# Three of sixteen weight units per feed-forward input step get their low parts from an accumulating DMA

## The reference

```python
h = rms_norm(x, norm_ffn[l])
gate_up = jnp.einsum('btd,df->btf', h, w_ffn_in[l])     # w_ffn_in: 2048 x 11264
ff_gate, ff_up = jnp.split(gate_up, 2, axis=-1)
x = x + jnp.einsum('btf,fd->btd', jax.nn.silu(ff_gate) * ff_up, w_ffn_out[l])
```

## Time and profile before

| | us |
|---|---|
| median of 3 runs | 2148.68 |
| lowest, highest run | 2147.15, 2149.55 |
| profiled execution, span of its instructions | 2146.8 |
| PE busy, all instructions | 2135.6 (99%) |
| DVE busy | 1742.5 (81%) |
| ACT busy | 1261.2 (59%) |
| POOL busy | 138.1 (6%) |

### The profile page before, as it was taken

The page is one execution under the profiler, slowest core; times in us unless marked ns, Lnnn a source line. Parts: engine busy times, 40 slices in busy tenths (PEclk is TensorE's granted clock), DMA queues, the critical chain, the costliest instruction groups (busy, mean ns, idle before and its releaser), DMA issues.

```text
span 2146.8 us, 30208 instructions
## 1 busy us (share of the span) xinstructions
PE 2135.6 (99%) x10176; PEld 1788.8 (83%) x10176; DVE 1742.5 (81%) x2125; ACT 1261.2 (59%) x1483; POOL 138.1 (6%) x218
## 2 busy tenths in 40 slices
PE   9999999999999999999999999999999999999998
PEld 9988888888888888888888888888888888888886
DVE  6578788666565698999899887787889999999886
ACT  6465455465544665555555555557667666666565
POOL 2022433101000000000000000000000000000000
PEclk9999999999999999999999999999999999999999
DMA  7666555575555566666666666666666666656664
GB/s 254 182 189 211 157 157 150 174 236 174 183 186 181 186 205 199 198 196 198 203 188 196 200 193 199 192 204 187 206 206 187 188 193 194 193 180 208 203 193 152
DMA packets 211513, 412.35 MB, mean 192 GB/s; under 512 B 13176, under 2 KB 13280, under 8 KB 211296
## 3 DMA queue, kind: packets, MB, share of 16 engines
q1 hardware_dynamic: 208608, 402.70, 60.9%
q0 software_dynamic: 1920, 5.31, 0.8%
q10 hardware_dynamic: 896, 3.15, 0.5%
HBM read 409.01 MB, written 3.16 MB: 192 GB/s over the span
## 4 chain that ended last, share of the span: by engine, by line
PE 96%; DVE 2%; DMA 1%; ACT 0%; issue 0%; DVEq 0%; SPq 0%; ACTq 0%
PE gp L1983 49%; PE gp L1915 33%; PE mx L1983 10%; PE mx L2226 1%; PE mx L2110 1%; DVE w_lo L1194 1%; DMA raw<-a_w_out_in 1%; PE mx L2275 1%; DVE t_lo L1426 0%; DVE ff_lo L1193 0%; PE mx L2113 0%; DMA x_tok<-x_in 0%; PE mx L2107 0%; PE mx L2162 0%; PE mx L2206 0%
## 5 line engine op out<-in xcount | busy, mean ns | idle before, releaser
L615 ACT ACTIVATE w_hi<-raw 128x1024 fp32r<-128x1024 f32 x759 | 797.1, 1056 | 681.6 <-PE gp L1915 246.3
L1194 DVE TENSOR_TENSOR w_lo<-raw,w_hi 128x1024 fp32r<-128x1024 f32 x759 | 921.2, 1230 | 233.8 <-ACT w_hi L615 224.1
L1983 PE MATMUL gp<-w_hi,a_hi 128*128 128x512 f32 x1053 | 413.3, 393 | 0.0
L1983 PE MATMUL gp<-w_lo,a_hi 128*128 128x512 f32 x1053 | 410.1, 389 | 0.0
L1983 PE MATMUL gp<-w_hi,a_lo 128*128 128x512 f32 x1053 | 409.8, 389 | 0.0
L1983 PEld LDWEIGHTS gp<-w_hi,a_hi 128*128 128x128 f32 x1053 | 197.7, 188 | 43.0 <-issue 2.9
L1983 PEld LDWEIGHTS gp<-w_lo,a_hi 128*128 128x128 f32 x1053 | 197.6, 188 | 41.4
L1983 PEld LDWEIGHTS gp<-w_hi,a_lo 128*128 128x128 f32 x1053 | 197.8, 188 | 39.8
L1915 PE MATMUL gp<-w_hi,a_hi 128*128 128x512 f32 x576 | 229.9, 399 | 0.0
L1915 PE MATMUL gp<-w_lo,a_hi 128*128 128x512 f32 x576 | 224.6, 390 | 0.0
L1915 PE MATMUL gp<-w_hi,a_lo 128*128 128x512 f32 x576 | 224.3, 389 | 0.0
(11 more groups left out here) (420 smaller groups left out, 3305.3 us busy)
## 6 DMA issues: line engine op xcount, KB each, us to landing
raw<-a_w_in_in SPq DMA_DIRECT2D x192, 512.0 KB, 4.5
raw<-w_ffn_in_in SPq DMA_DIRECT2D x176, 512.0 KB, 4.5
raw<-w_in_in SPq DMA_DIRECT2D x175, 512.0 KB, 3.9
raw<-w_ffn_out_in SPq DMA_DIRECT2D x88, 512.0 KB, 4.6
raw<-a_w_out_in SPq DMA_DIRECT2D x64, 512.0 KB, 4.9
raw<-w_out_in SPq DMA_DIRECT2D x32, 512.0 KB, 4.0
raw<-w_proj_a_in SPq DMA_DIRECT2D x16, 512.0 KB, 4.6
raw<-w_proj_b_in SPq DMA_DIRECT2D x16, 512.0 KB, 4.7
```

The source lines that it names most:

```text
L615: act.activation(w_hi[:, slot], raw[:, slot], ACT.Copy).then_inc(hi_ready, 1)
L1194: dve.tensor_tensor(w_lo[:, slot], raw[:, slot], w_hi[:, slot], ALU.subtract).then_inc(lo_ready, 1)
L1983: ins = pe.matmul(out_, stat[sp_], mov[mp], start=start and p == 0, stop=stop and p == 2, skip_group_check=True)
```

## The change

In steps of `FFN_IN` the units 7, 11 and 15 (`ADDED`; the odd units of plain pairs 3, 5 and 7, all in slot 3) get their low parts in another way. ACT first writes the negated high part, `w_lo = -raw` rounded to float32r, counts `neg_ready`, and then makes `w_hi` as before. POOL waits for `neg_ready` and issues a DMA with `accum_op=ALU.add` that adds `raw` to `w_lo` in place; its landing counts `lo_added[n]`. DVE only writes one number into a scratch column, to count `lo_ready` when the high part is there. PE issues the eight products with the unit's high part first, waits for `lo_added[n]`, and then issues the four with its low part. SP additionally waits for `lo_added[n]` before it loads the next unit into slot 3. SP's loops over the steps of `FFN_IN` and `FFN_OUT` are written out.

```diff
+ADDED = (7, 11, 15)
...
+        def added(k, unit):
+
+            return k == FFN_IN and unit in ADDED
...
                     if (k, i) != (0, 0) or j >= RING:
                         sp.wait_ge(lo_ready, after(k, i, j + 1 - RING))
+                    if added(k, j - RING):
+                        sp.wait_ge(lo_added[ADDED.index(j - RING)], i * 16 + 16)
+                    if k == FFN_IN and j == RING - 1 and i > 0:
+                        sp.wait_ge(lo_added[-1], i * 16)
+                    if (k, i, j) == (FFN_OUT, 0, RING - 1):
+                        sp.wait_ge(lo_added[-1], 16 * S[FFN_IN].steps)
...
             pool.dma_start(ws_raw[:], a_w_s.rearrange("g p q -> p g q")).then_inc(ws_in, 16)
+            for i in range(S[FFN_IN].steps):
+                for n, unit in enumerate(ADDED):
+                    pool.wait_ge(neg_ready, i * len(ADDED) + (n + 1))
+                    pool.dma_start(w_lo[:, unit % RING].bitcast(F32), raw[:, unit % RING], accum_op=ALU.add).then_inc(lo_added[n], 16)
...
-            def split(slot, use, used, tiles=None):
+            def split(slot, use, used, tiles=None, by_dma=False):
                 act.wait_ge(raw_in[slot], use)
                 if used is not None:
                     act.wait_ge(unit_used, used)
+                if by_dma:
+                    act.activation(w_lo[:, slot], raw[:, slot], ACT.Copy, scale=-1.0).then_inc(neg_ready, 1)
...
-            def split(slot, n, tiles=None):
+            def split(slot, n, tiles=None, by_dma=False):
                 dve.wait_ge(hi_ready, n)
+                if by_dma:
+                    dve.memset(small[:, 60:61], 0.0).then_inc(lo_ready, 1)
+                    return
...
+            def added_unit(k, i, u, half):
+
+                slot = (2 * u + half) % RING
+                for m in range(TB):
+                    for kk in range(UK):
+                        for stat in operand(k, i, u, kk, m):
+                            pe.matmul(gp[:, half, m], stat, w_hi[:, slot, kk], start=False, stop=False, skip_group_check=True)
+
+            def added_low(k, i, u, half):
+
+                slot, end = (2 * u + half) % RING, S[k].units - 1
+                pe.wait_ge(lo_added[ADDED.index(2 * u + half)], i * 16 + 16)
+                for m in range(TB):
+                    for kk in range(UK):
+                        ins = pe.matmul(gp[:, half, m], operand(k, i, u, kk, m)[0], w_lo[:, slot, kk], start=False,
+                                        stop=u == end and kk == UK - 1, skip_group_check=True)
+                    if u == end and m == 0:
+                        ins.then_inc(z_done, 1)
+                return ins
```

More of the change, by code:

```diff
@@ L239, in build @@
         lo_ready = sem("lo_ready")
+        neg_ready = sem("neg_ready")
+        lo_added = [sem(f"lo_added{n}") for n in range(len(ADDED))]
         unit_used = sem("unit_used")
@@ L501, in _ @@
                     load(k, 0)
+                    continue
+                if k in (FFN_IN, FFN_OUT):
+                    for i in range(S[k].steps):
+                        load(k, i)
                     continue
@@ L619, in ahead @@
                 n = unit0[k] + RING + j
-                split(j % RING, i * (16 * S[k].pair // RING) + 16 * (n // RING + 1), after(k, i, j + 1), tiles_ahead(k, i, j))
+                split(j % RING, i * (16 * S[k].pair // RING) + 16 * (n // RING + 1), after(k, i, j + 1), tiles_ahead(k, i, j),
+                      added(k, j + RING))
             def step(k, i, evac, last=False, mid=None):
@@ L1422, in double_ahead @@
                     weight_sums(k, i, mixed(k, i).index(u), j)
-                split(j % RING, after(k, i, RING + j + 1), tiles_ahead(k, i, j))
+                split(j % RING, after(k, i, RING + j + 1), tiles_ahead(k, i, j), added(k, j + RING))
                 if u in mixed(k, i) and half == 1:
@@ L2002, in plain_pair @@
                     pe.wait_ge(lo_ready, after(k, i, 2 * u + half + 1))
+                    if added(k, 2 * u + half):
+                        added_unit(k, i, u, half)
+                        ins = added_low(k, i, u, half)
+                        ins.then_inc(unit_used, 1)
+                        mid(i, 2 * u + half)
+                        continue
                     for m in range(TB):
```

## The result

The changed kernel takes 2187.89 us in the median of 4 runs (2184.13 to 2189.74), the kernel before 2148.15 (2147.15 to 2149.55). The ratio is 1.0184, with a 95% interval of 1.0169 to 1.0198: 39.7 us slower. It is within the range and on the side that was forecast, but little more than half of the 73 us. The profiled execution is the fastest of the four, with a span of 2182.5 us, 35.7 us longer than before (2146.8).

A forecast was written before the change was run, and what follows sets the result against it. The prediction took PE, busy 466.69 of 466.69 us in the feed-forward input windows, as the bound. The slot chain's 63 us plus step 0's 10 made 73, added to the median 2148.68 for 2222 us; range 2150 to 2310.

The forecast's parts named there:

- PE has nothing to gain: In the feed-forward input PE never idles, so relieving DVE of 40 us is worth 0; rival faster, at most 2147, chance 0.03.
- A = 7.1 us: Time from the end of ACT's negation to the add's landing: 6.9 us for the add, 0.2 for signals.
- The chain through slot 3 is not hidden: In steps 1 to 10, slot 3's loads wait for adds, costing 6.3 us a step, 63 us; chance 0.45.
- 27.5 + 3A: Time once round slot 3 in a step, with three adds: 48.8 us against 42.5 that PE needs.
- Step 0: First step of the feed-forward input: stalls of 5.0 us at unit 7, 2.5 each at 11 and 15, together 10.0.
- The covers: Loads of units 12 to 14, held behind SP's wait, stay covered by 2.4 us: worth 0; uncovered, about 30 us.
- The cheap add: Rival: an add costs no more than a plain copy, A = 5.4, 12 us plus 5 in step 0; 2166, chance 0.18.
- The dear add: Rival: the add takes 9.5 us, A = 9.7, 141 us plus 18 in step 0; 2308, chance 0.22.
- the rule of a fixed 2.0 us and the bytes at 436 GB/s: In the hidden-add rival (2151, chance 0.12): an add of two 512 KB reads takes 4.4 us, costing nothing.

The follow-up runs named there:

- the plain copy: The changed kernel with its 33 adds replaced by plain DMA copies of raw over w_lo, without the add; 2156.36 us, ratio 1.0039.
- the profile with a clean step 0: The changed kernel with POOL's load of ws_raw moved behind the stage's adds; 2186.63 us, ratio 1.0186.
- The old order of products: The changed kernel with all twelve products of each of the three units behind the wait for the add; 2191.45 us, ratio 1.0198.
- the run with two adds in slot 3: The changed kernel with only units 7 and 15 added, 11 by DVE, and ws_raw loaded behind the adds; 2166.33 us, ratio 1.0088.
- the adds of unit 10: From the changed kernel with units 7, 10 and 15 added in place of 7, 11 and 15; unit 10 lies in slot 2; 2203.24 us, ratio 1.0253.

## Why the prediction was right, and where its size was off

**PE has nothing to gain.** Right: DVE lost 37 us of work and no experiment came out faster than before. Those that hide the adds best end at 1.0019 to 1.0021.

**The price of an add, A = 7.1 us.** Right as a median (6.8 to landing, 0.3 signal), and the way to it, a plain DMA of this size plus a second read, is shown by the plain copy: 5.6 against 6.8. That the median was hit to 0.1 us is in part luck: the plain DMA took 0.4 more than the 5.2 of ws_raw, the second read 1.2 in place of 1.7. Wrong as a constant: 4.9 where the loads are held back, 7.4 where they run, 8.7 to 9.4 where an add left among loads just released.

**"The chain through slot 3 is not hidden."** The mechanism is shown. In every looped step the load of slot 3 leaves within 0.1 us of the landing of each add, and the negations of 11 and 15 follow their loads' landings as closely; taking the wait of the loads away brings back 32 of 40 us at landings that are no shorter; moving PE's need by 1.8 us changed nothing beyond the intervals. What the prediction had wrong is where PE feels it. It expected some 2 us of idle time before the low products of each of the three units, 33 times; the products waited twelve times, ten of them at unit 15. The lag of a round reaches PE mostly there and at the turn of the step, not in three equal parts.

**The size of the round is the term that was off:** 27.5 + 3A = 48.8 us forecast, 45.65 measured, so 3.2 us a step in place of 6.3. Link by link, at the median step: negation, signal and landing of the three adds 23.2 (24.5 forecast: the 4.9 of unit 11); from a landing to the next negation 3.9 twice (4.5: the first load of a queue that was held lands in 3.7, not 4.2); from the landing of 15 to the negation of 7, 14.5 (15.3). Three links each a little short, and since only what exceeds 42.5 counts, 6% of the round is half of the loss. I priced each link beside the loads of the kernel before. That the wait itself thins out those loads fits the landings of 3.7 and 4.9, but is argued, not tested by itself.

**Step 0, 10.0 us forecast, 6.6 measured.** The first stall was 2.35 us for 5.0 (the add landed in 6.2 us behind ws_raw, not in 8.6), unit 11 did not stall (landing 4.9), unit 15 did by 2.45. The clock, next, makes 1.7 more. Whether this sum may be added to the steps' stays open: the profile with a clean step 0 ended no earlier, but its steps were 0.4 us longer each, and its time is too near to tell.

**What was missing: the clock.** Behind some of the stalls the granted clock falls. Windows of the changed kernel (length, PE busy, weight loads, DVE, ACT, POOL, granted clock, DMA share, GB/s), around unit 15 of step 0:

```profile
776.00:780.00 4.00, 3.99 (x18) 2.98 (x16) 3.74 (x5) 2.04 (x4) 0.00 (x0) 1.00 0.90 215
780.00:784.00 4.00, 1.72 (x5) 1.34 (x6) 3.55 (x5) 2.05 (x2) 0.00 (x0) 0.81 0.26 44
784.00:788.00 4.00, 4.00 (x15) 3.23 (x14) 2.36 (x4) 2.83 (x5) 0.00 (x0) 0.76 1.01 378
788.00:792.00 4.00, 4.00 (x24) 3.38 (x23) 3.93 (x7) 0.92 (x1) 0.00 (x0) 1.00 0.82 266
```

The stall is at 780 to 782; then PE is busy 4.00 of 4.00 us, and the window holds 15 products where one at full clock holds 19 or 20 (a window of transposes more). The grant is 0.50, half of full speed (1.2 of 2.4 GHz), from 782.5 to 785.9, hence 0.76 in the mean of the window. The stage has three such stretches of 3.4 us, at 782.5, 874.7 and 966.8, behind stalls of products of 2.3, 2.3 and 1.8 us; each costs 1.7 us beside the stall itself, 5.1 together. The stalls of 2.2 us at 759 and at 1057 had none behind them, so the length of a stall alone does not tell. The old order of products lost 10 us in five stretches, one of them twice as long; the kernel before lost none in this stage.

**The covers.** SP's hold of the loads of 12 to 14 was worth 0 as said (DVE's waits for loads 10.7 us, 11.4 before). Not foreseen: DVE's product at the turn of a step comes late, and PE's transposes wait for it (5.9 us; their weight loads 8.4). It belongs to the same link, the one from the landing of 15: DVE makes it just after the low part of unit 3, whose load that landing releases. In the run with two adds in slot 3 a held load did reach the chain, so the cover was thin.

**The rivals.** The cheap add gave 2166; a DMA without the second read measured 2156. The dear add, 2308, rested on a landing of 9.5, which only the adds of unit 10 came near (9.4 at most), each among loads just released. By the rule of a fixed 2.0 us and the bytes at 436 GB/s (the Trainium skill, "DMA: Bandwidth & Descriptors", section "Anatomy of one DMA") an add is, as an estimate, 4.4 us; its shortest here is 4.9, in a quiet moment, its median 6.8.

What stays open: why the runs of one kernel with adds differ by 3 to 7 us among themselves, and which part of the last 4 to 5 us in the runs with one add a step is the held load and which DVE's queue. No version was found that beats the kernel before; with PE busy all of the stage there is no room for one unless DVE's spare time is given other work, which was not tried.

## What to carry to other kernels

Before an engine is relieved, look whether anybody waits for it: here PE was busy 100% of the stage, and 37 us of DVE's work were worth nothing. When a slow step is put on a buffer, follow the buffer once round, from use to reload to use, and compare that with the time that the bounding engine takes for it; the latency of the step alone says too little, and a few per cent of the round decide. A DMA's landing time belongs to the traffic beside it: price it as a range, and ask what its own landing will release into the next one.

## What the runs showed of the hardware

- An accumulating DMA from SBUF to SBUF, 512 KB, took 2.6 us of all 16 engines, a plain copy 1.3; issue to landing 4.9 to 8.2 us (median 6.8) against 3.8 to 7.0 (5.6). POOL's issue takes 0.86 us of its own time.
- An add that left within 0.7 us of three loads landed in 9.3 us, and the last of these loads took 9.2 (4.5 in the median before). In the steps 1 to 10 of that kernel the add in this place took 8.7 to 9.4.
- Three stalls of PE's products, of 2.3, 2.3 and 1.8 us, were followed by 3.4 us at half clock (grant 0.50), at a cost of 1.7 us each; two of 2.2 us in the same stage were not.
